# Two fp32 blocks on one core: first products inside the modulation, heads staged, attention over two projections, a third of the low parts on GpSimd

## What is computed

```
silu_c = silu(c); silu_cc = silu(c_ctx)
for l in range(2):
    shift, scale, gate       = split(silu_c  @ w_mod[l] + b_mod[l], 3)
    shift_c, scale_c, gate_c = split(silu_cc @ w_mod[l] + b_mod[l], 3)
    n  = rms_norm(h,  pre_norm_g[l]) * (1 + scale)   + shift
    nc = rms_norm(hc, pre_norm_g[l]) * (1 + scale_c) + shift_c
    p, pc = split(n @ w_in[l]), split(nc @ w_in[l])      # 14 chunks of 512 columns
    oa = diff_attention(q, k, v = p[0:3])    # 4 heads, each as two halves of 64, rotated, p1 - lam * p2, rms_norm
    ob = window_attention(p[3:6])            # 4 q heads, 2 k/v heads, rotated, masked, with a sink
    on = neighborhood_attention(p[6:9])      # 4 heads, bias, no rotation
    od = qknorm_attention(p[9:12])           # q and k normed, then rotated; 2 k/v heads
    y  = (concat(oa, ob, on, od) * silu(p[12])) @ w_out[l]
    h  = h + gate * rms_norm(y, post_norm_g[l])          # hc in the same way, in layer 0 only
```

## Time and profile before

| | us |
|---|---|
| median of 3 runs | 3254.26 |
| profiled execution | 3250.3 |
| its span | 3248.5 |
| PE busy | 2958.3 (91%) |
| DVE busy | 1950.4 (60%) |
| ACT busy | 1118.0 (34%) |
| POOL (GpSimd) busy | 247.4 (8%) |
| high parts, ACT L1885 | 656.6, 1053 ns each |
| low parts, DVE L1226 | 779.4, 1249 ns each |

### The profile page before, as it was taken

One profiled execution on the slowest core, in us unless ns is written; L12 is line 12 of the kernel. 1 busy time (PEld: TensorE's weight loads), 2 busy tenths in 40 slices (PEclk: granted clock), 3 DMA queues, 4 the chain that ended last, 5 costly groups with the idle time before them and its releaser, 6 DMA issues.

```text
span 3248.5 us, 40339 instructions
## 1 busy us (share of the span) xinstructions
PE 2958.3 (91%) x15557; PEld 2384.8 (73%) x15557; DVE 1950.4 (60%) x3426; ACT 1118.0 (34%) x1788; POOL 247.4 (8%) x269
## 2 busy tenths in 40 slices
PE   6889889999899979989998978878989999999998
PEld 1177567788678867767876767754688999999887
DVE  5377877676767754454253547777355666666444
ACT  2142322333223234333332433222343444444443
POOL 0000000000000000000001004545000000000000
PEclk9999899999999989999998988987698999999999
DMA  8855244454434533232332443321033555555555
GB/s 307 289 181 172 72 133 143 149 176 131 147 130 179 186 135 118 78 110 91 114 114 77 156 145 109 117 94 51 27 130 127 185 183 182 182 183 186 200 191 168
DMA packets 149808, 474.82 MB, mean 146 GB/s; under 512 B 16864, under 2 KB 17888, under 8 KB 148448
## 3 DMA queue, kind: packets, MB, share of 16 engines
q1 hardware_dynamic: 137664, 431.03, 40.2%
q10 hardware_dynamic: 9392, 32.30, 2.7%
q0 software_dynamic: 2560, 8.91, 0.9%
HBM read 459.07 MB, written 13.11 MB: 145 GB/s over the span
## 4 chain that ended last, share of the span: by engine, by line
PE 53%; issue 29%; DVE 9%; DMA 3%; POOL 2%; ACT 2%; ACTq 0%; DVEq 0%; POOLq 0%
PE bank L915 15%; PE bank L916 14%; PE bank L917 14%; DMA common<-w_mod 2%; PE bank L932 2%; PE bank L1097 1%; DVE split_weights L1226 1%; POOL common L2288 1%; PE bank L1019 1%; PE bank L1160 1%; PE bank L1112 1%; ACT split_weights L1885 1%; POOL first_block_work L2313 1%; PE bank L1000 1%; PE bank L1104 1%
## 5 line engine op out<-in xcount | busy, mean ns | idle before, releaser
L1226 DVE TENSOR_TENSOR split_weights<-common,split_weights 128x1024 fp32r<-128x1024 f32 x628 | 779.4, 1249 | 746.7 <-ACT split_weights L1885 680.6
L1885 ACT ACTIVATE split_weights<-common 128x1024 fp32r<-128x1024 f32 x628 | 656.6, 1053 | 1052.0 <-PE bank L917 986.9
L915 PE MATMUL bank<-split_weights,features 128*128 128x512 f32 x1920 | 803.6, 419 | 7.9 <-DVE features L1370 3.4
L917 PE MATMUL bank<-split_weights,features 128*128 128x512 f32 x1920 | 757.7, 395 | 0.0
L916 PE MATMUL bank<-split_weights,features 128*128 128x512 f32 x1920 | 757.3, 394 | 0.0
L915 PEld LDWEIGHTS bank<-split_weights,features 128*128 128x128 f32 x1920 | 366.5, 191 | 107.9 <-issue 30.9
L916 PEld LDWEIGHTS bank<-split_weights,features 128*128 128x128 f32 x1920 | 367.0, 191 | 77.9 <-issue 11.5
L917 PEld LDWEIGHTS bank<-split_weights,features 128*128 128x128 f32 x1920 | 365.7, 190 | 79.3
L915 PE MATMUL bank<-ffn_input_split,split_weights 128*128 128x256 f32 (+1 forms) x1376 | 392.9, 286 | 2.8 <-DVE ffn_input_split L1650 1.8
L916 PE MATMUL bank<-ffn_input_split,split_weights 128*128 128x256 f32 (+1 forms) x1376 | 391.5, 284 | 0.0
L917 PE MATMUL bank<-ffn_input_split,split_weights 128*128 128x256 f32 (+1 forms) x1376 | 391.1, 284 | 0.0
(11 more groups left out here) (279 smaller groups left out, 3336.0 us busy)
## 6 DMA issues: line engine op xcount, KB each, us to landing
common<-w_in SPq DMA_DIRECT2D x252, 512.0 KB, 3.3
common<-w_up SPq DMA_DIRECT2D x172, 512.0 KB, 4.2
first_block_work<-w_mod_cols SPq DMA_DIRECT2D x256, 256.0 KB, 3.7
common<-w_out SPq DMA_DIRECT2D x96, 512.0 KB, 3.3
common<-w_down SPq DMA_DIRECT2D x84, 512.0 KB, 3.3
common<-w_mod SPq DMA_DIRECT2D x64, 512.0 KB, 4.9
trig<-common ACTq DMA_DIRECT2D x32, 272.0 KB, 5.0
second_block_work<-trig POOLq DMA_DIRECT2D x32, 272.0 KB, 3.4
```

The costliest lines, as they stand in the source:

```text
L915: e.matmul(out_ap, xs[0], ws[0], start=first, stop=False)
L917: return e.matmul(out_ap, xs[0], ws[1], start=False, stop=last)
L1226: e.tensor_tensor(lo, raw, hi.bitcast(F32), ALU.subtract).then_inc(*low_done.tick(("lo", m)))
L1885: e.activation(split_slots[:, 0, i, 0:words], raw_slots[:, m % RAW, 0:words], ACT.Copy).then_inc(*high_done.tick(("high", m)))
```

## The change

- **First stage in quarters.** The 64 modulation pieces go through eight slots of their own (in the memory of the old stream), loaded by `mod_load_first`. Chunks are taken as shift, scale, shift, scale (0, 4, 1, 5, ...). After each pair, four feature blocks are scaled, modulated and split from rows transposed once after chunk 0 (`x_turn`, `normed_first`). The products of these blocks for diff's q (four tiles) and k (two latent tiles) stand among the modulation of the next quarter, two pieces each; the last four pieces stand behind `tables_end`. k's two context tiles are a projection of their own, for which k's eight pieces are loaded and split again.
- **Tables.** The angles are made by GpSimd, one table in two modulation pieces, with two buffers.
- **Staged heads.** The finished heads of tile t go to `stage[t]`, a part of `hid`, instead of the two row buffers; the sums of a rotation are made in place; `turn_a` and `turn_b` alternate. `turn_heads` is due 3 clocks (copy), 8 (rotation) or 14 (norm) after the finish instead of 3.
- **Order of groups.** diff, na, win, qk (`PLACES`), with the q of the second and the fourth in other memory. Each q projection is followed by `side_all`; a group's attention starts in its gate and runs on beside the next group's q. Pace 0.36 (layer 0) and 0.45 (layer 1) for the first three groups, 0.65 and 0.8 for the last.
- **Background** every 8 clocks while attention is in work, every 3 otherwise; layer 1's gate third last.
- **Low parts.** Every third piece of block 1 is subtracted by GpSimd (`on_gpsimd`).

```diff
-IN_ORDER = (0, 1, 2, 10, 3, 4, 11, 5, 6, 7, 12, 8, 9, 13)
+IN_ORDER = (0, 1, 2, 10, 5, 6, 7, 12, 3, 4, 11, 8, 9, 13)
+PLACES = (0, 2, 1, 3)
+MOD_SLOTS = 8
+MOD_ORDER = (0, 4, 1, 5, 2, 6, 3, 7)
-    plan = [A["w_mod"][c, g] for c in range(MOD_FIRST) for g in range(KT // KP)]
+    plan = [A["w_in"][0, c, g] for first in range(0, KT // KP, 2) for c in IN_ORDER[:2] for g in (first, first + 1)]
     for l in range(DEPTH):
-        for c in IN_ORDER:
+        for c in IN_ORDER[0 if l else 1:]:
+def on_gpsimd(m):
+    return m % 3 == 2 and m < (DEPTH * (INC + 4) + 1) * KT // KP
-GATE_PACE = (0.65, 0.8)
+PACE, LAST_PACE = (0.36, 0.45), (0.65, 0.8)
+TURN_AFTER = dict(copy=3, turn=8, norm=14)
...
-        if self.background and self.clock % 4 == 0:
+        if self.background and self.clock % (8 if self.side_work else 3) == 0:
...
+    def first_stage(self):
...
+        for i in range(4):
+            late = None
+            for c in (i, 4 + i):
+                for kg in range(KT // KP):
+                    self.do("mod_products", c, kg, done)
+                    done += 1
+                    self.mod_load()
...
+                            self.do("table_angles", step // 2)
+                            if step > 2:
+                                self.do("table", step // 2 - 1)
+                    if kg % 4 == 3 and pieces:
+                        self.first_products(*pieces.pop(0))
+                late = c
+                if c == 0:
+                    for f in range(KT):
+                        self.do("x_turn", f)
+                    self.weights()
+            self.do("mod_turn", late)
+            self.do("mod_scale", 0, i)
+            for f in range(4 * i, 4 * i + 4):
+                self.do("normed_first", f)
+                if f % 4:
+                    self.do("normed_first_split", f - 1)
+            self.do("normed_first_split", 4 * i + 3)
+            pieces = [(p, tiles, bank, kg) for p, tiles, bank in ((q, range(NT), 0), (k, range(LT), NT))
+                      for kg in (2 * i, 2 * i + 1)]
+        for j in range(step // 2, SJ):
+            self.do("table", j - 1)
+            self.do("table_angles", j)
+        self.do("table", SJ - 1)
+        self.do("tables_end")
+        for piece in pieces:
+            self.first_products(*piece)
...
-            self.turned.append((self.clock + 3, ("turn_heads", l, g, part, nh, t, r)))
+            self.turned.append((self.clock + TURN_AFTER[after], ("turn_heads", l, g, part, nh, t, r)))
...
         first = self.unit
         self.unit += len(units)
+        self.group_ends[(l, PLACES.index(g))] = self.unit - 1
         combine = None
+        while self.turned:
+            yield
...
-                if part == "q":
+                if l == 0 and g == 0 and part in "qk":
+                    if part == "k":
+                        self.project(tiles[LT:], self.heads(l, g, kind, "k", HEADS))
+                elif part == "q":
                     self.project(qtiles, self.heads(l, g, kind, "q", HEADS))
+                    self.side_all()
...
-            self.pace = GATE_PACE[l]
+            self.pace = PACE[l] if place < 3 else LAST_PACE[l]
             self.project(qtiles, self.gate(l, g))
-            self.pace = 1.0
-            self.side_all()
...
+        def low(m):
+            if not on_gpsimd(m):
+                return
...
+            e.tensor_tensor(lo, raw, hi.bitcast(F32), ALU.subtract).then_inc(*low_done_too.tick(("lo", m)))
...
+        def table_angles(j):
...
+            for s_ in range(2):
+                e.tensor_scalar(x[:, s_, :], steps_row, ssm_ph[:, j:j + 1], 0.25 * (1 - s_), ALU.mult, ALU.add).then_inc(
+                    *tables_reduced.tick())
+            e.wait_ge(*tables_reduced.last())
+            e.tensor_scalar(trig_w, x, HALF_UP, -HALF_UP, ALU.add, ALU.add).then_inc(*tables_reduced.tick())
+            e.wait_ge(*tables_reduced.last())
+            e.tensor_tensor(x, x, trig_w, ALU.subtract).then_inc(*tables_reduced.tick(("table_angles", j)))
...
-        def rotate_heads(nh, rope, p, t, bank, r, x, z):
+        def rotate_heads(l, nh, rope, p, t, bank, r, x, z):
...
-            a, b, dst = (halves(v[:, 0:w], half) for v in (turn_a, turn_b, rows_buf[r % 2]))
+            a, b = (halves(v[:, 0:w], half) for v in (stage[t], (turn_a, turn_b)[x % 2]))
```

More of the change, by code:

```diff
@@ L267, in take @@
                 self.finish_split()
-        if n >= MOD_PIECES and n not in self.split_have:
+        if n not in self.split_have:
             self.finish_split()
@@ L304, in rows, with turns @@
         return r
+    def turns(self, n=1):
+        self.turn += n
+        return self.turn - n
     def copies(self):
@@ L340, in whole @@
         return self.steps
+    def first_stage(self):
+        self.feature_set = ("normed", 0)
+        self.turns(2)
+        step, self.mod_loaded, done = 0, 0, 0
+        q, k = self.projections, self.projections + 1
+        self.projections += 2
+        for _ in range(MOD_SLOTS):
+            self.mod_load()
+        pieces = []
+        for i in range(4):
[4 more added lines that the diff above has]
+                    done += 1
+                    self.mod_load()
+                    if late is not None and kg == 1:
+                        self.do("mod_turn", late)
+                        late = None
+                    if i or c:
+                        step += 1
+                        if step % 2:
+                            self.do("table_angles", step // 2)
[8 more added lines that the diff above has]
+                    self.weights()
+            self.do("mod_turn", late)
+            self.do("mod_scale", 0, i)
[13 more added lines that the diff above has]
+            self.first_products(*piece)
@@ new lines, in mod_load, with first_products @@
+    def mod_load(self):
+        if self.mod_loaded < MOD_PIECES:
+            self.do("mod_load_first", self.mod_loaded)
+            self.mod_loaded += 1
+    def first_products(self, p, tiles, bank, kg):
+        finish = self.heads(0, 0, "diff", "q" if bank == 0 else "k", HEADS)
+        m = self.take()
+        for t in tiles:
+            for k in range(KP):
+                self.do("products", self.feature_set, p, t, bank + t, kg, k, m, t == tiles[-1] and k == KP - 1)
+                self.side()
+            if kg == KT // KP - 1:
+                finish(p, t, bank + t)
+            self.side()
@@ L371, in normed @@
     def normed(self, l):
-        self.turn += 1
-        x = self.turn
+        x = self.turns(2)
         for f in range(KT + 1):
```

329 lines of the change are left out of this document (204 added, 125 removed).

## The result

The changed kernel takes 3281.93 us (median of 4 runs, 3279.57 to 3282.34) against 3254.35 us of the kernel before, measured beside it: ratio 1.0081, 95% interval 1.0069 to 1.0092. It is slower by 27.6 us, where 3179 us was predicted. Its profiled execution has a span of 3280.3 us.

A forecast was written before the change was run, and what follows sets the result against it. Block 1 was taken as PE-bound wherever nothing is late, so only other stretches counted; terms of -26, -20, -6, -11, -5, -1, -4, -2.5, -3, +3 and 0 gave -75.5 us, hence 3179 us, range 3137 to 3230.

The forecast's parts named there:

- k's turns: Head transposes after k projections: coming due 8 or 14 clocks later, under the gate's products, they would cost no waits.
- Attention spread, -20, -6 and -11: Attention over gate and next q: -20 us layer 0 diff gate, -6 win gate, -11 layer 1's diff and win gates.
- The forecast's mark, under 10 us in the diff gate: Sign in the diff gate: PE's waits on DVE's combination of the two softmaxes would be under 10 us.
- the bare turns: After q projections, `side_all` issues head turns without products between; normed q idles 10.8 us in layer 1, 12.6 in layer 0.
- Head staging, -5, -1, -4, -2.5, -3, +3: Qk groups -5 and -1 us (layers 0, 1), win q and kv -4 and -2.5, layer 1 diff q and k -3, na q +3.
- the term for the clock (7): Layer 0's qk group: 7 us left for the slowed clock, within 12.6 + 9 + 7 replacing 33.7.
- the tail: The last attention starts 14 clocks late and its rest runs bare, about 5 us in layer 0, 9 in layer 1.
- Low parts on GpSimd, 0 (bounds -15, +90): 98 block 1 low parts on GpSimd, 2.4 us each: DVE's 1.25 us relief and the lock's holds cancel.
- the 15 named: Sign of being wrong: PE waiting for GpSimd's lows by over 15 us in all.
- 89 us: Slower rival's cost: 37 lows under attention each hold DVE 2.4 us, all passed to PE.
- First stage, -26: Start to diff v: 252 instead of 278.4 us, bounds -8 and -42, including a 12 us stall before the last k pieces.
- The slower rival: GpSimd's lock holds DVE under attention, costing 89 us against a gain of 75: 3268 us, chance 0.07.

The follow-up runs named there:

- e2: The changed kernel with the background at one advance in four clocks everywhere, as before the change: 3245.90 us, ratio 0.9974.
- e7: The kernel before with only the background changed, to one advance in 8 clocks beside attention and one in 3 otherwise: 3309.03 us, ratio 1.0178.
- e3: The changed kernel with all low parts on VectorE and the background at one advance in four clocks: 3234.17 us, ratio 0.9935.
- e1: The changed kernel with every low part on VectorE: 3258.89 us, ratio 1.0016.
- e5: e3 with only the attention drained after a q projection, the head turns waiting for k's products: 3201.00 us, ratio 0.9841.
- e8: e3 with the tables' angles made by VectorE instead of GpSimd: 3226.37 us, ratio 0.9916.
- e12: The changed kernel loading only the first three column pieces and multiplying all 256 background pieces from them (wrong weights): 3252.29 us, ratio 0.9990.
- e10: e3 with q's turns under products, last pace 0.8 and 1.2, angles on VectorE, background one in 6 beside attention, one in 4 otherwise: 3174.84 us.

## Why the prediction was wrong

**The step that failed** is the cadence of the background. The prediction used one half of it (fewer advances beside attention, "0.7 background turns" per unit) and never costed the other, one advance in three clocks elsewhere. It could have been done from the rows at hand: three clocks of layer 0 are 3 x 0.69 = 2.08 us, an advance for both streams two products of 0.75 us with 0.08 us reads, 1.67 us, and a low part of 1.25 us every 8 clocks (5.55 us), two in three of them on VectorE, adds 0.31: 1.98 us of VectorE in 2.08, before any copy or norm. And the column loads share SyncE's order with weight loads that wait for their slots. "Where a stall goes, say what is late next" was asked of the attention, not of the projections between: for the plain ones the sum has no term but k's turns ("block 1 is bound by PE wherever nothing is late; the sum is about the other stretches"), and they measured +28.1 us in place of about -7. Price of the cadence: 36 us of the time by e2, +55 us alone in e7. By the table the spans missed the forecast by 107 us: 35 in the plain projections, 16 in the qk gate, 13 each in the first stage and in layer 1's groups, 11 in diff gate and na q, 7 in the second block, 12 in the rest.

**Attention spread, -20, -6 and -11.** Wrong by itself too. With the cadence and the lock out (e3), diff gate and na q stand at 148.5 us, 7.1 below before, not 18.5, and the other pairs and the qk gate gain nothing. (e3 also advances the background twice as often beside the attention as the forecast assumed; in e1, where it goes as assumed, the two stand at 145.9, 9.7 below.) The waits for the combination moved rather than went: 16.4 us in one stretch became 5.2 and 5.9 in two. The forecast's mark, under 10 us in the diff gate, was met, and did not show that the second part of the attention waits again in na q. In layer 1 all groups together gave 2.8 us of the 16 forecast; with the q turns under products (e5) they fall by 18.5 more, so there the bare turns took back what spreading gave.

**Head staging, -5, -1, -4, -2.5, -3, +3.** The k turns' waits vanished, as said. The two bare normed q were priced nearly right as idle time (12.4 us in layer 1, 13.6 in layer 0, against 10.8 and 12.6), and the second tile of layer 1 did end 2.6 us sooner (2.5):

```profile
1734.22 0.60 ACT L2151 ACTIVATE common<-bank 128x512 f32<-128x512 f32 x1 [0.24 <-PE bank L1019]
...
1741.59 1.12 PE L1094 MATMUL bank<-common,first_block_work 128*128 128x128 f32 x4 [6.05 <-POOL first_block_work L2496]
...
1746.91 1.11 PE L1094 MATMUL bank<-common,first_block_work 128*128 128x128 f32 x4 [4.20 <-POOL first_block_work L2496]
```

In layer 1 the qk group's 31 us became 31.7 (23.3 idle, 8.4 of clock), where 29.8 was forecast. In layer 0 its 33.7 became 59.5 (37.1 idle, 22.4 of clock), where 28.6 was forecast: the term for the clock (7) was a third of what a group at 0.89 to 0.91 costs, and kv and gate idle 11.4 and 12.1 us against 9 for the tail. I also took the bare turns as a price to be paid; e5 shows what that choice of the change costs over all groups, 33 us.

**Low parts on GpSimd, 0 (bounds -15, +90).** Duration as worked out: 2.40 us median against 2.4. The lock as read in the earlier trace rows: a product of 0.75 us beside a low part takes up to 2.98. What was wrong is that nothing would be left: 23 us in the changed kernel, 12 with a background of one in four, 7 to 9 elsewhere; never below zero in four comparisons. The balance on VectorE, where relief and lock were to cancel, was even better than forecast (28 to 39 us less busy time); the cost came by ways that the term did not have; the traces show later column pieces and, in the changed kernel, later low parts of VectorE, and not how much of the time is each one's. TensorE waited only 0.3 us for GpSimd's low parts themselves, far from the 15 named. That it is no 89 us was right.

The Trainium skill, "SBUF — State Buffer", section "Who interferes with whom", says that a VectorE instruction with two SBUF inputs contends with a GpSimd instruction that reads SBUF. It calls the contention an exclusive lock, and says of VectorE's two-port modes that the engine that issues second is blocked for the whole of the other's instruction. The rows at 557.15 and 557.49 us agree with such a lock for the two-input product too: it started second and ended 0.55 us after GpSimd's low part, where it takes 0.75 alone.

**First stage, -26.** -13.4. The schedule held: last modulation product at 194.6 us (191), first weight product at 65.8 (60), and the hole before the last two k pieces came, 16.5 us (12, bounds 5 to 20). It ends at 230.4, and most of it has the predicted reason, GpSimd's angles for the last tables and the stores behind them:

```profile
214.33 0.96 POOL L2474 TENSOR_SCALAR common<-first_block_work,common 128x272 f32<-128x272 f32 x2
...
215.38 2.03 POOL L2477 TENSOR_SCALAR common<-common 128x544 f32<-128x544 f32 x1
217.49 1.33 POOL L2479 TENSOR_TENSOR common<-common 128x544 f32<-128x544 f32 x1
218.85 0.66 ACT L2051 ACTIVATE common<-common 128x544 f32<-128x544 f32 x1 [3.81 <-POOL common L2479]
219.54 0.33 ACTq L2054 DMA_DIRECT2D trig<-common  x1
222.04 2.00 ACT L2020 ACTIVATE split_weights<-common 128x1024 fp32r<-128x1024 f32 x2 [2.52 <-DMA trig<-common]
223.35 2.34 POOL L2462 TENSOR_TENSOR split_weights<-common,split_weights 128x1024 fp32r<-128x1024 f32 x1 [4.53 <-ACT split_weights L2020]
224.27 2.50 DVE L1341 TENSOR_TENSOR split_weights<-common,split_weights 128x1024 fp32r<-128x1024 f32 x1 [18.82 <-ACT split_weights L2020]
...
226.69 0.68 DVE L1569 TENSOR_TENSOR first_block_work<-bank,first_block_work 128x512 f32<-128x512 f32 x1
...
229.60 1.12 PE L1094 MATMUL bank<-common,first_block_work 128*128 128x128 f32 x4 [15.29 <-POOL first_block_work L2496]
```

A table's angles take 4.5 us of GpSimd (4.6 was the upper estimate); the high parts start at 222.0 us, where the whole split was expected by 218, and VectorE's low part beside GpSimd's takes 2.50 us. The split is done at 226.8; the last 3 us of the hole have a reason that the prediction did not name: before the k pieces stands the first turn of q's heads (229.60), whose rotation on VectorE (226.69) came only behind that low part. The rest is a few us everywhere: the quarter's start, the two waits for features (3.6 us), and the clock of 0.73 in the hole. Angles on VectorE give 7.1 us of it back (e8).

**The rivals.** The slower rival came true in sign and named GpSimd's lock; the whole offload is 12 to 23 us of the 103 between forecast and result, and the rival's sum (3268) is near the time for the wrong reason. None of the rivals held the cadence.

**Open.** Whether a deeper ring for the column pieces, or another place for their loads, gives e12's 27 us back was not run. How the cost of the offload divides between the lock and the later pieces is open too. What decides between some 1331 and some 1339 us in the second block: GpSimd, the pace and the angles each go with both levels, and e12's executions spread as far by themselves.

## What to carry over

Work that fills gaps on a side engine has a rate as well as a sum: when its cadence is changed, cost it in every stretch where it runs, per piece of the main work, and look at its loads, since in one program's list of loads they stand behind whatever waits for the main stream. An operation moved to GpSimd took 1.25 us each off VectorE and cost time in all four comparisons: the sum of busy time fell, but what stood beside and behind the moved operation came later. A drain with no products behind it ("until both lists are empty") is worth replacing by one that drains only what the next step needs.

## What the runs showed of the hardware

- GpSimd's subtraction of 128 x 1024 words: 2.34 to 3.42 us, median 2.40, against VectorE's 1.23. With VectorE's product of 128 x 512 (0.75 us) started beside it the product takes up to 2.98 us.
- A GpSimd one-input operation on 128 x 544 words took 2.03 us and a two-input one on the same size 1.33 us (rows above): my assumption in the prediction that one-input operations may be quicker held at 272 words (0.48 us each, against 0.73 for two inputs at 256) and not at 544.
- The second block, with the same instructions, took 1330 to 1332 us in eight profiled executions and 1337 to 1342 in six. The granted clock over it was 0.90 in the changed kernel and 0.91 before and in e10. Since the executions of one kernel spread too (e12), these levels are not shown to belong to a version of block 1.
